# First sums, decays and B·C products made one stage earlier, and products with the identity where TensorE waits

## What is computed

```python
hc = ctx * (1 + mods_c[1]) + mods_c[0]         # modulation, also h = x * (1 + sc1) + sh1
proj_c = hc @ w_in[l]
...
a_cum = jnp.cumsum(dtc * a, axis=2)            # per chunk and head: the "sums"
states = jnp.einsum("bcsgn,bcsgrp->bcgrpn", bc, (decay_to_end * dtc)[..., None] * xc)
h_last, h_in = lax.scan(step, h0, ...)
...
seg = a_cum[:, :, :, None] - a_cum[:, :, None, :]
decay = jnp.exp(jnp.where(lower, seg, -jnp.inf))
cb = jnp.einsum("bclgn,bcsgn->bclsg", cc, bc)  # the B·C products
wgt = cb[..., None] * decay * dtc[:, :, None]
y = jnp.einsum("bclsgr,bcsgrp->bclgrp", wgt, xc)
y = y + jnp.einsum("bclgn,bcgrpn->bclgrp", cc, h_in) * jnp.exp(a_cum)[..., None]
...
out = sum over chosen experts of gate * gelu(u_tab[idx] . h2) * v_tab[idx]
```

## Time and profile before

| what | us |
|---|---|
| median of 3 runs | 4710.15 (4709.54 to 4715.5) |
| profiled execution | 4699.58 |
| its span | 4697.8 |

### The profile page before, as it was taken

One profiled execution on the slowest core, in us unless ns is written; L12 is line 12 of the kernel. 1 busy time (PEld: TensorE's weight loads), 2 busy tenths in 40 slices (PEclk: granted clock), 3 DMA queues, 4 the chain that ended last, 5 costly groups with the idle time before them and its releaser, 6 DMA issues. The chain is left out here.

```text
span 4697.8 us, 48345 instructions
## 1 busy us (share of the span) xinstructions
PE 3419.5 (73%) x15506; PEld 1711.8 (36%) x15506; DVE 3161.5 (67%) x6602; ACT 1551.7 (33%) x3816; POOL 2038.8 (43%) x1555
## 2 busy tenths in 40 slices
PE   7788888897789976555678566888996555555555
PEld 5586324332476333111234113767732111111111
DVE  5355787664666677777766776676666677677775
ACT  4452344343352234222222323374222222222221
POOL 0063454543023544555444451024345555555554
PEclk8899999999799988777899777989998777777777
DMA  5647999999555999999999995263599999999998
GB/s 206 212 156 279 405 421 402 420 426 393 212 169 219 407 398 418 411 423 420 404 425 425 399 419 209 91 203 109 190 402 408 411 413 421 420 418 419 413 419 370
DMA packets 275698, 1618.74 MB, mean 345 GB/s; under 512 B 47010, under 2 KB 61154, under 8 KB 87653
## 3 DMA queue, kind: packets, MB, share of 16 engines
q0 software_dynamic: 184320, 1342.26, 69.0%
q1 hardware_dynamic: 91124, 273.39, 16.1%
HBM read 1594.21 MB, written 21.33 MB: 344 GB/s over the span
## 5 line engine op out<-in xcount | busy, mean ns | idle before, releaser
L2660 PE MATMUL banks<-arena 128*64 128x512 f32 x5120 | 1568.6, 748 | 1018.3 <-ACT arena L2419 1015.7
L2129 POOL DMA_INDIRECT arena<-in_experts,arena x1280 | 1512.1, 1181 | 1671.1 <-PE banks L2660 1418.2
L2252 DVE CUSTOM_DVE_ANT_0 arena<-arena,token_copies 128x1024 f32<-128x1024 f32 x1280 | 1642.9, 1301 | 700.8 <-DMA arena<-in_experts,arena 637.2
L2660 PEld LDWEIGHTS banks<-arena 128*64 128x64 f32 x5120 | 376.9, 163 | 2011.1 <-ACT arena L2419 1397.7
L2412 ACT ACTIVATE arena<-arena 128x2 f32<-128x2 f32 x640 | 131.2, 205 | 1734.3 <-DVE arena L2252 1729.9
L2419 ACT ACTIVATE arena<-arena 128x64 f32<-128x64 f32 x1280 | 376.5, 340 | 277.8 <-POOL arena L1953 237.3
L301 POOL TENSOR_TENSOR wide_low<-wide_blocks,wide_high 128x1024 fp32r<-128x1024 f32 x88 | 218.1, 2501 | 294.7 <-ACT wide_high L290 250.6
L2475 PE MATMUL banks<-arena,wide_blocks 128*128 128x512 f32 (+3 forms) x960 | 309.7, 471 | 10.7 <-ACT arena L2281 8.1
L954 POOL TENSOR_TENSOR arena<-arena 128x1024 f32<-128x1024 f32 x20 | 39.3, 1990 | 552.2 <-POOLq L833 483.2
L2550 PE MATMUL banks<-arena,wide_blocks 128*128 128x512 f32 x576 | 276.9, 618 | 0.0
L339 PE MATMUL banks<-activation_a,wide_high 128*128 128x256 f32 (+1 forms) x768 | 258.3, 336 | 23.2 <-DVE arena L1404 12.1
(11 more groups left out here) (265 smaller groups left out, 4723.1 us busy)
## 6 DMA issues: line engine op xcount, KB each, us to landing
wide_blocks<-in_wide SPq DMA_DIRECT2D x182, 1024.0 KB
arena<-cum_rows SPq DMA_DIRECT2D x80, 256.0 KB, 3.5
arena<-in_experts,arena POOLq DMA_INDIRECT x1280
pre_scan<-arena SPq DMA_DIRECT2D x16, 256.0 KB
arena<-pre_scan SPq DMA_DIRECT2D x16, 256.0 KB, 5.4
residual<-in_tokens SPq DMA_DIRECT2D x6, 512.0 KB, 6.9
arena<-mod_rows SPq DMA_DIRECT2D x6, 512.0 KB
norm_rows<-in_keys SPq DMA_DIRECT2D x3, 1024.0 KB
```

The costliest lines, as they stand in the source:

```text
L2129: pool.indirect_dma_start(out=v.ring[:, g % RING], out_offset=None, in_=io["experts"], in_offset=bass.IndirectOffsetOnAxis(ap=c.idx[:, u % ...
L2252: last = nc.vector.tensor_tensor_reduce(out=u_row, in0=u_row, in1=k.copies[:, n % NJ], scale=1.0, scalar=0.0, op0=ALU.mult, op1=ALU.add, a ...
L2660: mm = nc.tensor.matmul(k.ps[j * QUAD:(j + 1) * QUAD, a + half], v.lhs[:, g % 4, j], v.ring[:, (g * NJ + j) % RING, D + half * BANK:D + (h ...
```

## The change

- In `stage_states`, SP loads the sums of the first four units (`load_sums`), behind the keeping of the sums and ahead of the last weight load and the last kept rows; ACT makes the decays of units 0 and 1 (`unit_decays`) between two turns of the modulation, or at once where there are none; PE makes the B·C products of chunk 0 (`products_bc`) at its end, ahead of `finish_used`.
- `stage_outputs` leaves these out. The sums' buffers, the decay tiles and DVE's two scratch rows move within the scratch so that they can be written in the earlier stage. `intra` waits for the xd of its own direction alone.
- `turn_tokens`, `modulate` and `modulate_rest` use four banks. Of every second column block ACT makes only the rounded one, and DVE makes the raw one from PSUM and subtracts. PE may transpose block kt when block kt-4 is through DVE. The merge's wait before its first product is gone.
- `keep_busy` issues products of the 128x128 identity with itself, whose result nobody reads: six before the first `intra` of each output stage, twenty at the end of layer 0's latent outputs, eight at the end of reload, sixteen at the start of finish, eight behind the first transposes of each retrieval, and five behind the products of ranks 4, 5 and 6 in the last unit of each retrieval.

```diff
+EARLY_UNITS = 2
+def keep_busy(k, bank, count):
+    for _ in range(count):
+        k.nc.tensor.matmul(k.ps[:, bank, 0:P], k.ident[:], k.ident[:], start=True, stop=True)
...
 def turn_tokens(k, pe, NT, tb):
     for kt in range(KT):
-        if kt >= 2:
-            pe.wait_ge(k.h_hi.sem, k.h_hi.at(kt - 1))
+        if kt >= 4:
+            pe.wait_ge(k.h_ready.sem, k.h_ready.at(kt - 3))
         for t in range(NT):
-            last = k.nc.tensor.transpose(k.ps[:, kt % 2, t * P:(t + 1) * P],
+            last = k.nc.tensor.transpose(k.ps[:, 4 + kt % 4, t * P:(t + 1) * P],
...
 def modulate(k, act, v, T, at=0):
-        if kt >= 2:
-            act.wait_ge(k.h_ready.sem, k.h_ready.at(kt - 1))
-        for dst, sig in ((k.act_a[:, kt, at:at + T], None), (v.hraw[:, kt % 2, at:at + T], k.h_hi)):
...
+        k.nc.scalar.activation(k.act_a[:, kt, cols], k.ps[:, 4 + kt % 4, 0:T], ACT.Identity, bias=shift, scale=scale) \
+            .then_inc(k.h_hi.sem, 1)
+        if kt % 2 == 0:
+            if kt >= 2:
+                act.wait_ge(k.h_ready.sem, k.h_ready.at(kt - 1))
+            k.nc.scalar.activation(v.hraw[:, 0, cols], k.ps[:, 4 + kt % 4, 0:T], ACT.Identity, bias=shift, scale=scale) \
+                .then_inc(k.h_raw.sem, 1)
...
 def modulate_rest(k, dve, v, low, T, at=0):
     for kt in range(KT):
+        if kt % 2 == 0:
+            dve.wait_ge(k.h_raw.sem, k.h_raw.at(kt // 2 + 1))
+        else:
+            dve.drain()
+            dve.wait_ge(k.h_hi.sem, k.h_hi.at(kt + 1))
+            k.nc.vector.tensor_scalar(v.hraw[:, 1, cols], k.ps[:, 4 + kt % 4, 0:T], v.modc[:, 1, kt:kt + 1],
+                                      v.modc[:, 0, kt:kt + 1], ALU.mult, ALU.add)
+            dve.drain()
...
 (stage_states, SP)
             if mods:
+                load_wides(k, sp, w0 + 2 + WIDE_SLOTS)
+            if rows:
+                sp.wait_ge(k.cum_kept.sem, kept0 + 16)
+                for n in range(4):
+                    load_sums(k, sp, v, n, 0, 0, n)
+            if mods:
                 load_wides(k, sp, w0 + mods.count + WIDE_SLOTS)
                 mods.keep(sp, 0)
-            if rows:
-                sp.wait_ge(k.cum_kept.sem, kept0 + 16)
 (stage_states, ACT)
-            for i in range(mods.count + 1 if mods else 0):
+            turns = mods.count + 1 if mods else 0
+            for i in range(turns):
                 mods.take(act, i)
+                if rows and i - turns // 2 in range(EARLY_UNITS):
+                    unit_decays(k, act, v, i - turns // 2, 0, 0, i - turns // 2, row0)
+            if rows and not mods:
+                for n in range(EARLY_UNITS):
+                    unit_decays(k, act, v, n, 0, 0, n, row0)
 (stage_states, PE)
+            if rows and mods:
+                pe.wait_ge(k.mod_used.sem, k.mod_used.at(-1))
+            if rows:
+                products_bc(k, v, 0, 6)
             if mods:
                 finish_used(k, pe)
...
+def sum_rows(v):
+    return v.scr[:, 4096:6144].rearrange("p (a h c) -> p a h c", a=4, h=HPG)
+def decay_tiles(v):
+    return [v.scr[:, at:at + BANK].rearrange("p (h c) -> p h c", h=HPG) for at in (6144, 6656, 3072, 3584)]
+def load_sums(k, sp, v, n, t, d, g):
+    h0 = d * 16 + g * HPG
+    sp.dma_start(sum_rows(v)[:, n % 4].rearrange("p h c -> p (h c)"),
+                 k.io["cum"][t, h0:h0 + HPG].rearrange("h c -> (h c)").unsqueeze(0).to_broadcast([P, HPG * P])) \
+        .then_inc(k.sums_landed[n % 4].sem, 16)
+def unit_decays(k, act, v, n, t, d, g, row0):
+    act.wait_ge(k.sums_landed[n % 4].sem, row0[n % 4] + 16 * (n // 4 + 1))
...
+    k.nc.scalar.activation(tile, tile, ACT.Exp, scale=-1.0).then_inc(k.decay_ready.sem, 1)
+def products_bc(k, v, t, bank):
+    for gg in range(GROUPS):
+        last = k.nc.tensor.matmul(k.ps[:, bank, gg * P:(gg + 1) * P], v.BT[:, gg, t * P:(t + 1) * P],
+                                  v.CT[:, gg, t * P:(t + 1) * P], start=True, stop=True)
+    last.then_inc(k.cb_ready.sem, 1)
...
 (stage_outputs)
-    ysum = s[:, 5120:5120 + D]
-    ytmp = s[:, 6144:6144 + D]
+    ysum = s[:, 1024:1024 + D]
+    ytmp = s[:, 2048:2048 + D]
                 if n >= 4:
                     sp.wait_ge(k.seg_ready.sem, k.seg_ready.at(n - 3))
...
+                    load_sums(k, sp, v, n, t, d, g)
-                pe.wait_ge(k.xd_ready.sem, k.xd_ready.at(2 * t + 2))
+                pe.wait_ge(k.xd_ready.sem, k.xd_ready.at(2 * t + d + 1))
-            both(0)
+                if n == 0:
+                    keep_busy(k, INT + 1, 6)
                 intra(n)
+            if squares_here:
+                keep_busy(k, CB, 20)
+                if n >= EARLY_UNITS:
+                    unit_decays(k, act, v, n, t, d, g, row0)
...
 (stage_merge, PE)
             turn_tokens(k, pe, NT - kept // P, tb + kept // P)
-            pe.wait_ge(k.h_hi.sem, k.h_hi.at(KT))
 (stage_reload, PE, last)
+            keep_busy(k, 7, 8)
 (stage_finish, PE, first)
+            keep_busy(k, 6, 16)
 (stage_peer, PE, behind the first transposes)
+                keep_busy(k, 6, 8)
 (stage_peer, PE, behind each rank)
+                        if u == UNITS - 1 and RANKS // 2 <= q < RANKS - 1:
+                            keep_busy(k, 6, 5)
```

51 lines of the change are left out of this document (21 added, 30 removed).

## The result

The changed kernel takes 4685.35 us (median of 5 runs, 4677.13 to 4688.95), the one before 4709.54 beside it (5 runs, 4707.13 to 4715.5). The ratio is 0.9941, with a 95% interval of 0.9930 to 0.9952: 24.2 us less, where 24.7 had been forecast. A second set of runs of the changed kernel (the experiment e12) has a median of 4682.79 (7 runs, 4662.69 to 4686.38) and a ratio of 0.9947 (0.9934 to 0.9960).

A forecast was written before the change was run, and what follows sets the result against it. Stage times add; transfers bound the untouched retrievals, and dead time opening the output stages was the largest thing touched. Outputs -17.5, states +5.0, modulation -7.8 and identity-product terms sum to -24.7 us: median 4685.5, range 4672 to 4699, with rivals 4664 to 4704.

The forecast's parts named there:

- Outputs: Three output stages: early sums, decays and B·C products let PE start sooner, -17.5 us (-28.5 to -3.0).
- The other price: Start of output stages: DVE's masks held by POOL's xd products, about one mask for each, 1.87 us apiece.
- States: States' stages: cost of four early sums, a later weight load and B·C products, +5.0 us (0 to +8.2).
- Layer 0's +1.05: Layer 0's states, context and latent: B·C products delay the last weight load and stage end, +1.05 us each.
- Modulation: Two projections and two merges: shared columns, four banks, no merge wait, -7.8 us (-4.0 to -9.5).
- Reload's eight: Eight identity products at reload's end, for the first work of the states: -0.8 us (-1.6 to +1).
- Finish: Sixteen identity products at the start of finish, while PE waits for DVE: -0.5 us (-1 to +1).
- Starts of the retrieval: Eight identity products in each retrieval's opening gap: 0.9 us in each latent, 0.7 in the context's, -2.5 in all.
- Ends of the retrieval: Fifteen identity products while PE waits for ACT, before the last products: -0.8 us (-1.6 to +1).
- one of my signs of being wrong: Retrieval stages that move by over 3 us, which no step of the prediction gives.
- given back: Rival: POOL holds masks, first unit without early sums waits, clock rises no sooner; -7 us, 4703; chance 0.17.
- Slower: Rival: identity products don't raise the clock and run at 1.2 GHz themselves; +18 us, 4728; chance 0.06.

The follow-up runs named there:

- e12: The changed kernel, unchanged, run again for a second profile and more runs: 4682.79 us, ratio 0.9947.
- e1: The kernel before with only the new modulation (four banks, shared raw columns, no merge wait): 4703.71 us, ratio 0.9999.
- e2: The changed kernel without any of its identity products: 4693.55 us, ratio 0.9969.
- e7: The changed kernel with chunk 0's B·C products back at the start of the output stages: 4682.47 us, ratio 0.9947.
- e10: As e9, with PE giving the weight slot back ahead of the B·C products in the states' stages: 4673.00 us, ratio 0.9930.
- e8: The kernel before, unchanged, run again for a second profile: 4706.36 us, ratio 1.0005.
- e3: The changed kernel with a transpose of the identity in place of each identity product: 4686.82 us, ratio 0.9954.
- e5: The changed kernel with no early decays in the states' stages (sums and B·C products stay there): 4687.71 us, ratio 0.9959.
- e9: As e4, without the six identity products ahead of each output stage's first unit: 4678.88 us, ratio 0.9931.
- e4: The changed kernel with three of POOL's first x times dt products waiting for masks 2, 5 and 6: 4671.86 us, ratio 0.9924.
- e11: The same kernel as e4, run again: 4668.95 us, ratio 0.9910.

## Why the prediction was right, point by point

The sum stands by the medians: 24.2 against 24.7. That it stands to half a microsecond is luck, since its terms are off by more. They are set here against the means of the two profiles of each kernel:

- **Outputs, forecast -17.5, measured -23.7** (context -9.8, layer 0 -8.0, layer 1 -5.9). Direction, place and order of size were right; the term was too small. The price that was off is that of the start: I put PE's opening at 1.2 GHz (4.9 us; its two parts, 1.94 and at most 2.8, give 4.7), since it had been so before. In the changed kernel's first profile it is at 2.4 in all three stages, the modulation product and the six take 2.6, and the first unit starts 2.5 us in. Only in layer 1 of e12 was it at 1.2 (4.2 us in). The other price, 1.87 us a mask beside POOL, was 2.3. And I had no term for what came behind it: PE's waits for these masks are followed by a spell at 1.2 GHz, 3.4 us in layer 0 and 17 in the context's outputs (6.8 in e12), where chunk 0 ended 26.5 us in (21.6 in e12; I had 21 to 24). In layer 0 it ended 20.9 us in.
- **In the context that gain can't all be put down to the early start.** e1, with no early start at all, has outputs of 50.8 there and 188.6 in the three stages together; the changed kernel has 189.3 and 184.5, e2 188.2. So in the context the early start with its sums is worth between +0.7 and -4.1, the rest can't be told from where the clock fell in these executions. In the latent stages e1 shows 90.3 and 87.5, and e2, with the early start and no identity products, 83.7 and 81.0: there the gain is the early start's.
- **States, forecast +5.0, measured +3.4 in the context, -0.3 in layer 0, -0.2 in layer 1.** The sums in the context's queue of weight loads cost about what I said: PE's waits for weight blocks grew by 2.5 us, where I had 2.9. Layer 0's +1.05 is there too (e7: 1.4 less without it, e10: 0.9), balanced by the start at full clock. One reading was wrong, without effect: ACT isn't idle all of layer 1's states but for 22.2 of 23.5 us (25.84 less the 3.64 in the next stage).
- **Modulation, forecast -7.8, measured -9.6** (context's project -1.4 and merge -3.3, layer 1's project -3.3 and merge -1.5). In the context's merge it is nearly as worked out (four pairs at 1.5 us instead of 1.9 save 1.6, not the 1.4 that I took). Layer 1's project gained more than the -0.9 to -1.3 of its pace, and its two profiles differ by 2.5; why isn't shown. In layer 1's merge the first product comes 2.9 us sooner, and half of that is lost behind it; a part of the loss is PE's wait of 0.89 for a subtraction that ran beside POOL's cutting, a bound that I had named only for the masks.
- **Identity products.** Reload's eight and the states: 1.2 us at the start of the states, 0.8 forecast. Twenty at the end of the outputs: hidden. Finish -0.45, forecast -0.5. Starts of the retrieval, -1.7, -1.0 and -2.4 until the first gather, so -5.0 where I had -2.5 (the kernel before's own two profiles differ by 1.8 in the last of them; the context's 0.7 had been a guess). Ends of the retrieval, forecast -0.8: in the first profile the context's last products are at half clock as before, with a gap of 2.97 us ahead of them, 3.53 before; in e12 they are at full clock behind 3.21, 1.6 us less. So it comes in one execution and not in the other. Taken together, e2 puts them at 8.2 us in the medians.
- **Retrieval.** No step touched its transfers; it swings by 10 to 13 us between executions of one kernel. A retrieval that moves by over 3 us was one of my signs of being wrong; it moved by 10 us in the first profile, but between the two of the kernel before as well, so the sign says nothing. My sum went from one profile to the median of runs by carrying the difference of 10.6 us along; I didn't ask where it came from, and the short retrieval of that execution (10.3 under e8's) covers it.

Of the rivals, "given back" was the nearest to happen: POOL does hold the masks, the fifth unit's sums are late by 2.47 us, and without the identity products the clock does fall. "Slower" is refuted by e2 and, in the latent retrievals, by e3: what stands in the gaps does hold the clock. In e5 and e9, without the early decays and without the six, chunk 0 went to 1.2 GHz; but in e10, also without the six, it didn't in the context and in layer 0, and in the changed kernel itself it did for a while. So the six aren't shown to be needed for the clock, and for the early decays there is e5 alone.

What stays open: with two profiles for a kernel, whose stages outside the retrieval differ by 9.6 us, the terms for the context are known to about 4 us and those elsewhere to 1 or 2. The terms measured add up to more than the medians show. A part of this is the second profile of the changed kernel, the fastest execution of its set; by the first alone the stages outside the retrieval are 26.6 shorter than the mean of before. And what makes the clock fall in one execution and not in the other is open.

## What to carry to other kernels

Ask of an engine that starts earlier what it then runs into: here POOL's products, which had been harmless while DVE had nothing to do, became the next wait, and putting them behind the masks (three waits on POOL, e4 and e11) gave another 14.5 us. A few products that nobody reads were worth their time here where they closed a short gap in front of dense work (8.2 us in all, e2); behind a gap of some 3 us they helped in one of two executions. And compare stage by stage, with two profiles of each kernel: a stage can move by 5 us with the clock between two executions of one kernel, and one execution's retrieval hides a change of this size. One run without a thing shows little where the clock swings like this: by e9 alone the six would look indispensable, but e10 lacks them too and took 4673.00, beside 4670.0 with them.

## What the runs showed of the hardware that I had not expected

- Where the clock was at 2.4 GHz, transposes of the identity held it as well as products of twice their time (e3: 3.81 us for layer 1's first queries with either, 6.40 with neither). Where it was at 1.2, in the context's retrieval, eight of them didn't raise it in time: 5.86 us, and 3.84 behind the products.
- A wait of PE of 1.4 to 1.7 us among the first products of a stage was followed by a stretch at 1.2 GHz, in which PE was busy for 8.73 and 9.67 of 10.1 us (e5, e9); without that wait the same work ran at 2.4 GHz (e4). It isn't a rule: behind the same wait of 1.42 us it ran at 2.4 GHz in e10.
- A POOL product and a VectorE product with both operands in SBUF slow each other: four of each took 8.8 and 8.6 us side by side; apart, four POOL products took 7.5, and four masks would take 2.8 (0.69 each).
- The same instructions of the context's outputs took 56.3 or 50.8 us in two kernels that differ only ahead of them (e8, e1), and 49.0 or 44.1 in two executions of one kernel (after, e12), with the clock over the stage at 0.67 and 0.74, 0.72 and 0.82.
